# A two-layer kernel on one core: row norms by halves, the root on ScalarE, a Newton step on VectorE

## The chip, the core and the metric

One core of a Trainium2 chip runs the whole program. The time is that of the device for one execution, in microseconds; a median of several runs is given. TensorE (PE) does matmuls and transposes, ScalarE (ACT) functions by table, VectorE (DVE) element-wise work, GpSimd (POOL) the same more slowly, SyncE (SP) issues most transfers. Each engine runs its own instructions in order and waits on semaphores for the others.

## The reference

Two layers on 256 rows of 1024 floats, float32 throughout. What the change touches is the row norm, which stands at six places:

```python
def rmsnorm(x, g):
    y = xf * lax.rsqrt(jnp.mean(xf * xf, axis=-1, keepdims=True) + EPS)
    return (y * g).astype(x.dtype)

h = rmsnorm(x, g_pre)                       # "x"; the projections h @ w_in follow
cross_mixer(q, z, rmsnorm(mem, g_mem), ...) # "m"
x = x + rmsnorm(merged @ w_o, g_post)       # "wo", and the residual sum: end of layer 1
h = rms_norm(x, mix_norm_gain)              # "y": layer 2 begins, projections follow
x = x + mixed @ w_out
h = rms_norm(x, ffn_norm_gain)              # "f": gate/up projections and w_down follow
out = rms_norm(x + ffn, final_norm_gain)    # "o"
```

Between these stand gated linear attention, sparse and cross attention in layer 1, and a gated delta rule with a convolution, block-compressed attention and a feed-forward part in layer 2.

## The kernel before

The 256 rows are two row tiles (t = 0, 1) of 128 partitions by 1024 columns; `xres` holds the residual rows and `xn` the normed or scratch rows. A product with fp32 accuracy is made of three matmuls (L486 to L488): activations and weights are each split into a rounded high part and a low rest. The weights stream through a ring of five slots, a "unit" of up to 2048 columns at a time. For each unit ACT writes the high part (`highs`, L1288) and DVE the low one (`lows`, L1762), in the order of the list `splits`, some two units ahead of PE. `highs(n)` and `lows(n)` do what is missing up to the nth; `bank_ready(name)` does this for two units beyond the bank's own and then waits for the bank. `step(ins)` lets an engine wait for its own instruction.

Products of 512 columns fill the eight PSUM banks in a fixed rotation. A product of row tiles t and column half c has the name `wo<c><t>` (w_o), `w2o<c><t>` (w_out) or `wd<c><t>` (w_down): half 0 of both row tiles is finished first, then half 1.

A norm goes through four engines. ACT squares 1024 columns of one row tile and sums them (`squares`, L1271, instruction at L1273) once all are there; POOL turns the sum into mean plus epsilon (L1665) and raises it to -1/2 (L1666); DVE scales the row tile (`scale_rows`, L1788, instruction at L1791); PE transposes both row tiles (`transpose_tokens`, L542, L551), eight transposes of 128 columns each; the first bank is full after two of the second row tile's. ACT and DVE then write high and low parts of the transposed rows (`high_of_transposed`, L1305; `low_of_transposed`, L1793). PE's order has nothing between the product before a norm and the transposes behind it, except at "m".

In the middle ACT copies the four banks of w_o into `xn` (L1303), squares, and POOL makes the factor of "wo". DVE multiplies by factor and gain (L2046) and adds to `xres` (L2047), and on that sum the "y" norm is made. Behind it ACT has Exp of a small tile (L1497), the high parts of units c1 and c2, and the copies into the convolution, whose taps DVE does at L2099 and L2101. At "f" and "o" DVE adds the banks to `xres` (L2352, L2381) and the norm follows; at the end it multiplies by factor and gain (L2385), and SP stores each row tile (L1234), 512 KB, as it is ready. The order of all this is written out by hand on each engine.

## Time and profile before

| | us |
|---|---|
| median of 3 runs | 953.02 (952.66 to 954.28) |
| the profiled execution | 951.25 |
| its span, first to last instruction | 949.5 |

| Engine | busy us | share |
|---|---|---|
| PE | 907.9 | 96% |
| DVE | 560.5 | 59% |
| ACT | 427.4 | 45% |
| POOL | 60.6 | 6% |

Busy time says which engine works; what ends last is read from the chain of waits. In a timeline a row gives the start, the time from the first start to the last end, the engine, the line and the shape, and in brackets how long the engine had been idle and who released it. Lines are those of the kernel before.

### The profile page before, as it was taken

To read this page: it belongs to the slowest core of one execution; us is meant where nothing else is said; L and a number is where in the kernel's file an instruction comes from. 1 tells how busy PE (TensorE), PEld (TensorE's weight loads), DVE (VectorE), ACT (ScalarE), POOL (GpSimd) and SP (SyncE) were. 2 spreads that over 40 slices of the span, in tenths; PEclk is the share of its full clock that TensorE was granted. 3 is DMA by queue.
4 is the path that set the end of the run, shared out by engine and by line. 5 is a ranking of instruction groups with operands and counts; after the bars stand their busy time and mean duration, and the time that the engine had idled before them with its cause. 6 is when DMAs were issued, how large, how long until landed. Compare 5 with 4: busy or idle time off the path is not lost.

```text
span 949.5 us, 13232 instructions
## 1 busy us (share of the span) xinstructions
PE 907.9 (96%) x5502; PEld 793.6 (84%) x5502; DVE 560.5 (59%) x802; ACT 427.4 (45%) x568; POOL 60.6 (6%) x72
## 2 busy tenths in 40 slices
PE   6999999999999999999699999899989899999996
PEld 5999999899897888887599998677877788888885
DVE  4855564664567565655579786645276555566442
ACT  6644445644346444433554424553443444444341
POOL 1000000000020000000201253000000000000000
PEclk9999999999999999999899999999999999999999
DMA  9657643455264455466567453003563456665441
GB/s 303 196 177 233 201 165 133 134 177 174 94 222 150 161 177 178 152 225 197 165 178 176 91 149 119 1 1 133 133 222 133 155 178 180 191 193 191 155 155 45
DMA packets 127490, 151.77 MB, mean 160 GB/s; under 512 B 16919, under 2 KB 93078, under 8 KB 127430
## 3 DMA queue, kind: packets, MB, share of 16 engines
q1 hardware_dynamic: 127290, 150.83, 50.2%
q8 instruction: 44, 0.72, 0.3%
q14 instruction: 16, 0.13, 0.1%
q0 software_dynamic: 64, 0.07, 0.0%
q10 hardware_dynamic: 76, 0.02, 0.0%
HBM read 148.80 MB, written 3.68 MB: 161 GB/s over the span
## 4 chain that ended last, share of the span: by engine, by line
PE 88%; DVE 8%; ACT 2%; issue 1%; POOL 0%; DMA 0%; ACTq 0%; POOLq 0%; DVEq 0%
PE bank L486 24%; PE bank L487 24%; PE bank L488 24%; DVE w_lo L1762 2%; DVE arena L2101 1%; PE bank L551 1%; PE bank L926 1%; PE bank L957 1%; PE bank L911 1%; PE bank L921 1%; PE bank L731 1%; ACT w_hi L1288 1%; PE bank L900 1%; PE bank L632 1%; PE bank L612 1%
## 5 line engine op out<-in xcount | busy, mean ns | idle before, releaser
L1762 DVE TENSOR_TENSOR w_lo<-ring,w_hi 128x2048 fp32r<-128x2048 f32 (+2 forms) x133 | 299.7, 2258 | 196.6 <-ACT w_hi L1288 196.4
L1288 ACT ACTIVATE w_hi<-ring 128x2048 fp32r<-128x2048 f32 (+2 forms) x133 | 250.0, 1881 | 140.4 <-PE bank L488 128.4
L486 PE MATMUL bank<-h_hi,w_hi 128*128 128x256 f32 (+1 forms) x640 | 184.8, 289 | 2.7 <-DVE w_lo L1762 1.4
L487 PE MATMUL bank<-h_lo,w_hi 128*128 128x256 f32 (+1 forms) x640 | 181.8, 284 | 0.0
L488 PE MATMUL bank<-h_hi,w_lo 128*128 128x256 f32 (+1 forms) x640 | 181.7, 284 | 0.0
L486 PE MATMUL bank<-w_hi,h_hi 128*128 128x512 f32 (+1 forms) x400 | 155.7, 389 | 0.8 <-DVE h_lo L1799 0.8
L488 PE MATMUL bank<-w_hi,h_lo 128*128 128x512 f32 (+1 forms) x400 | 152.7, 382 | 0.0
L487 PE MATMUL bank<-w_lo,h_hi 128*128 128x512 f32 (+1 forms) x400 | 152.5, 381 | 0.0
L486 PEld LDWEIGHTS bank<-h_hi,w_hi 128*128 128x128 f32 (+1 forms) x640 | 123.1, 192 | 5.7 <-issue 3.3
L487 PEld LDWEIGHTS bank<-h_lo,w_hi 128*128 128x128 f32 (+1 forms) x640 | 123.1, 192 | 0.7 <-issue 0.5
L488 PEld LDWEIGHTS bank<-h_hi,w_lo 128*128 128x128 f32 (+1 forms) x640 | 123.0, 192 | 0.0
L1303 ACT ACTIVATE arena<-bank 128x512 f32<-128x512 f32 (+4 forms) x86 | 47.7, 568 | 118.9 <-PE bank L488 95.5
L486 PEld LDWEIGHTS bank<-w_hi,h_hi 128*128 128x128 f32 x400 | 75.2, 188 | 15.9 <-issue 1.8
L488 PEld LDWEIGHTS bank<-w_hi,h_lo 128*128 128x128 f32 x400 | 75.2, 188 | 14.7
L487 PEld LDWEIGHTS bank<-w_lo,h_hi 128*128 128x128 f32 x400 | 75.3, 188 | 13.7
L1335 ACT ACTIVATE arena<-bank 128x512 f32<-128x512 f32 (+1 forms) x48 | 23.9, 500 | 96.5 <-PE bank L488 96.4
L1665 POOL TENSOR_SCALAR arena<-arena 128x1 f32<-128x1 f32 (+2 forms) x17 | 5.3, 313 | 678.0 <-ACT arena L1273 378.1
L486 PE MATMUL bank<-w_hi,y_hi 128*128 128x512 f32 x96 | 39.0, 406 | 1.2 <-DVE w_lo L1762 1.2
L487 PE MATMUL bank<-w_lo,y_hi 128*128 128x512 f32 x96 | 37.9, 395 | 0.0
L1456 ACT ACTIVATE arena<-arena 128x128 f32<-128x128 f32 (+1 forms) x48 | 21.3, 445 | 36.6 <-DVE arena L1978 36.6
L488 PE MATMUL bank<-w_hi,y_lo 128*128 128x512 f32 x96 | 37.7, 393 | 0.0
L487 PE MATMUL bank<-w_lo,f_hi 128*128 128x512 f32 x88 | 35.1, 399 | 0.0
(312 smaller groups left out, 1270.3 us busy)
## 6 DMA issues: line engine op xcount, KB each, us to landing
ring<-in_w_in SPq DMA_DIRECT2D x60, 1024.0 KB, 4.9
ring<-in_w_gate_up SPq DMA_DIRECT2D x44, 512.0 KB, 4.6
ring<-in_w_down SPq DMA_DIRECT2D x10, 1024.0 KB, 5.0
ring<-in_w_mem_kv SPq DMA_DIRECT2D x8, 1024.0 KB, 7.1
ring<-in_w_gla_out SPq DMA_DIRECT2D x4, 1024.0 KB, 4.9
ring<-in_w_x_out SPq DMA_DIRECT2D x4, 1024.0 KB, 5.0
ring<-in_w_dsa_out SPq DMA_DIRECT2D x4, 1024.0 KB, 5.1
ring<-in_w_o SPq DMA_DIRECT2D x4, 1024.0 KB, 5.0
```

What stands on the lines that cost most here:

```text
L486: mm(o, ah, bh, start=start, stop=False, skip_group_check=True)
L487: mm(o, ah, bl, start=False, stop=False, skip_group_check=True)
L488: return mm(o, al, bh, start=False, stop=stop, skip_group_check=True)
L551: ins = nc.tensor.transpose(bank_of(f"T{tag}{j}")[:, 256 * kk + 128 * t:256 * kk + 128 * t + 128], src[:, t, 128 * k:128 * k + 128], ident)
L612: ins = mm(bank[:, 256 * t:256 * t + 256], xq[:, 2 * h + c, 128 * t:128 * t + 128], mk[:, 2 * h + c, :], start=c == 0, stop=c == 1)
L632: ins = mm(bank[:, 256 * c:256 * c + 256], mv[:, m, at:at + 128], probT[:, h % 3, 256 * m:256 * m + 256], start=m == 0, stop=m == 1)
L731: ins = nc.tensor.transpose(bank[:, a:a + 128], rows[:, a:a + 128], ident)
L1288: act(w_hi[:, k % NHI, 0:m], ring[:, order.index(name) % NSLOT, 0:m], ACT.Copy)\
L1303: act(dst, src, ACT.Copy, scale=1.0 if scale is None else scale).then_inc(inc or bank_reader(name), 1)
L1335: act(tnh[:, i % 2, 0:n], src, ACT.Tanh, scale=0.5).then_inc(inc or signal("tanh_done"), 1)
L1456: ins = act(v, v, ACT.Exp, bias=neg_max[:, c:c + 1], scale=-1.0, accum_out=p_sum[:, c:c + 1])
L1762: tt_(w_lo[:, i, 0:m], ring[:, i, 0:m], w_hi[:, k % NHI, 0:m].bitcast(F), ALU.subtract)\
```

## The change

For x and m: ACT squares a row tile as before and then takes the square root of mean plus epsilon itself; DVE makes the same mean, the reciprocal of the root, and one Newton step as a correction factor (1.5 - 0.5 r v r), and scales by both factors in one instruction. The wait for and copy of the parameters `par0` moves behind x's scaling on DVE, and ACT waits for it.

For wo, y, f and o: the sum of squares comes in two halves of 512 columns. The first half's mean (`first_half`, DVE) is the bias under the second half's root. For wo the squares are read from the banks, ACT's copies go, DVE multiplies each bank by the gain (`wo_gain`), and factor and residual sum are one instruction for each half. At the end the gain is multiplied in before the factor is known, and each row tile is scaled and stored in two halves, four transfers of 256 KB. `load_root_table` is a root of no use that stands early, so that the table is there. POOL's work for these norms goes; it writes the constant `eps`. SP's store of the middle rows waits for four halves (`x_mid` 4). Left out below: the counts of waits, POOL's removed lines (one is shown), and the definition of `eps`.

```diff
+                act(p_inv[:, col + t:col + t + 1], sumsq[:, col + t:col + t + 1], ACT.Sqrt, scale=1 / D, bias=eps)\
+                    .then_inc(signal(f"root_{tag}"), 1)
+            square_count = {}
+            def half_squares(tag, src, col, c, t):
+                n = square_count[tag] = square_count.get(tag, 0) + 1
+                i = col + 2 * c + t
+                act(probT[:, c, :], src, ACT.Square, accum_out=sumsq[:, i:i + 1]).then_inc(signal(f"sumsq_{tag}"), 1)
+                sc.wait_ge(signal(f"sumsq_{tag}"), n)
+            def root(tag, col, t):
+                sc.wait_ge(signal(f"first_{tag}"), t + 1)
+                act(p_inv[:, col + 2 + t:col + 3 + t], sumsq[:, col + 2 + t:col + 3 + t], ACT.Sqrt, scale=1 / D,
+                    bias=var[:, col + t:col + t + 1]).then_inc(signal(f"root_{tag}"), 1)
+            def load_root_table():
+                step(act(p_inv[:, 15:16], eps, ACT.Sqrt))
...
+            sc.wait_ge(signal("eps"), 1)
             for t in range(TT):
                 squares("x", xres, 0, t, (signal(f"x_in{t}"), 16))
             highs(1)
+            sc.wait_ge(*read("par0"))
...
-            copy_wide("wo0", xn, 0)
-            for t in range(TT):
-                copy(f"wo1{t}", xn[:, t, 512:1024])
-                squares("wo", xn, 4, t, read(f"wo1{t}"))
-            highs(splits_by["wo11"] + 2)
-            for t in range(TT):
-                squares("y", xres, 0, t, (signal("x_mid"), t + 1))
+            def y_squares(t):
+                for c in range(2):
+                    sc.wait_ge(signal("x_mid"), 2 * t + c + 1)
+                    half_squares("y", xres[:, t, 512 * c:512 * c + 512], 0, c, t)
+                root("y", 0, t)
+            for t in range(TT):
+                bank_ready(f"wo0{t}")
+                half_squares("wo", bank_of(f"wo0{t}")[:, :], 4, 0, t)
+            load_root_table()
+            for t in range(TT):
+                bank_ready(f"wo1{t}")
+                half_squares("wo", bank_of(f"wo1{t}")[:, :], 4, 1, t)
+                root("wo", 4, t)
+                if t == 0:
+                    highs(splits_by["wo11"] + 2)
+            for t in range(TT):
+                y_squares(t)
...
-            highs(splits_by["w2o11"] + 2)
-            for t in range(TT):
-                squares("f", xres, 4, t, read(f"w2o1{t}"))
+            load_root_table()
+            highs(splits_by["w2o01"] + 2)
+            for c in range(2):
+                for t in range(TT):
+                    sc.wait_ge(*read(f"w2o{c}{t}"))
+                    half_squares("f", xres[:, t, 512 * c:512 * c + 512], 4, c, t)
+                    if c == 1:
+                        root("f", 4, t)
+                highs(splits_by["w2o11"] + 2)
...
+            load_root_table()
             highs(len(splits))
-            for t in range(TT):
-                squares("o", xres, 6, t, read(f"wd1{t}"))
+            for c in range(2):
+                for t in range(TT):
+                    sc.wait_ge(*read(f"wd{c}{t}"))
+                    half_squares("o", xres[:, t, 512 * c:512 * c + 512], 0, c, t)
+                    if c == 1:
+                        root("o", 0, t)
...
-                rsqrt_mean("o", 6 + t, 1, D, t + 1)
...
-            def rstd_of(tag, col, t):
-                ve.wait_ge(signal(f"rstd_{tag}"), t + 1)
-                return rstd[:, col + t:col + t + 1]
+            def rstd_of(tag, col, t, n, before):
+                i = slice(col + t, col + t + 1)
+                ve.wait_ge(signal(f"sumsq_{tag}"), n)
+                if before is not EPS:
+                    ve.wait_ge(signal(f"first_{tag}"), t + 1)
+                step(tsc(var[:, i], sumsq[:, i], 1 / D, before, ALU.mult, ALU.add))
+                ve.wait_ge(signal(f"root_{tag}"), t + 1)
+                step(nc.vector.reciprocal(rstd[:, i], p_inv[:, i]))
+                step(stt(p_sum[:, i], rstd[:, i], var[:, i], rstd[:, i], ALU.mult, ALU.mult))
+                step(tsc(p_sum[:, i], p_sum[:, i], -0.5, 1.5, ALU.mult, ALU.add))
+                return rstd[:, i], p_sum[:, i]
+            def scale_tile(tag, src, dst, col, t, n, before):
+                r, correction = rstd_of(tag, col, t, n, before)
+                tsc(dst[:, t, :], src[:, t, :], r, correction, ALU.mult, ALU.mult).then_inc(signal(f"scaled_{tag}"), 1)
+            def first_of(col, t):
+                return var[:, col + t:col + t + 1]
+            def first_half(tag, col, t, n):
+                ve.wait_ge(signal(f"sumsq_{tag}"), n)
+                tsc(var[:, col + t:col + t + 1], sumsq[:, col + t:col + t + 1], 1 / D, EPS, ALU.mult, ALU.add)\
+                    .then_inc(signal(f"first_{tag}"), 1)
 
             def scale_rows(tag, dst, src, col):
                 for t in range(TT):
-                    r = rstd_of(tag, col, t)
-                    tsc(dst[:, t, :], src[:, t, :], r, None, ALU.mult).then_inc(signal(f"scaled_{tag}"), 1)
+                    scale_tile(tag, src, dst, col, t, t + 1, EPS)
...
+            scale_rows("x", xn, xres, 0)
             ve.wait_ge(*full("par0"))
             nc.vector.tensor_copy(par[:, 0:38], bank_of("par0")[:, 0:38]).then_inc(reader("par0"), 1)
             ve.wait_ge(*read("par0"))
             tsc(g_gla_half, g_gla, 0.5, None, ALU.mult)
-            scale_rows("x", xn, xres, 0)
...
+            def wo_gain(c, t):
+                s = slice(512 * c, 512 * c + 512)
+                tt_(xn[:, t, s], bank_of(f"wo{c}{t}")[:, :], g_post[:, s], ALU.mult).then_inc(reader(f"wo{c}{t}"), 1)
+            def x_in_the_middle(t):
+                r, correction = rstd_of("wo", 6, t, 3 + t, first_of(4, t))
+                step(tt_(r, r, correction, ALU.mult))
+                for c in range(2):
+                    s = slice(512 * c, 512 * c + 512)
+                    ve.wait_ge(*read(f"wo{c}{t}"))
+                    stt(xres[:, t, s], xn[:, t, s], r, xres[:, t, s], ALU.mult, ALU.add).then_inc(signal("x_mid"), 1)
+            ve.wait_ge(signal("g_post_in"), 16)
+            for t in range(TT):
+                bank_ready(f"wo0{t}")
+                first_half("wo", 4, t, t + 1)
+                wo_gain(0, t)
             lows(splits_by["wo11"] + 2)
-            ve.wait_ge(signal("g_post_in"), 16)
             ve.wait_ge(signal("x_again"), 16)
             for t in range(TT):
-                r = rstd_of("wo", 4, t)
-                step(stt(xn[:, t, :], xn[:, t, :], r, g_post, ALU.mult, ALU.mult))
-                tt_(xres[:, t, :], xres[:, t, :], xn[:, t, :], ALU.add).then_inc(signal("x_mid"), 1)
-            scale_rows("y", xn, xres, 0)
+                ve.wait_ge(signal("sumsq_wo"), 3 + t)
+                wo_gain(1, t)
+                x_in_the_middle(t)
+                first_half("y", 0, t, 2 * t + 1)
+                if t == 1:
+                    ve.wait_ge(signal("x_mid"), 4)
+                    scale_tile("y", xres, xn, 2, 0, 2, first_of(0, 0))
+            scale_tile("y", xres, xn, 2, 1, 4, first_of(0, 1))
...
+                    if c == 0:
+                        first_half("f", 4, t, t + 1)
             ve.wait_ge(*read("w2o11"))
-            lows(splits_by["Tf3"] + 2)
-            scale_rows("f", xn, xres, 4)
+            for t in range(TT):
+                scale_tile("f", xres, xn, 6, t, 3 + t, first_of(4, t))
...
+                    ve.wait_ge(*read(f"wd{c}{t}"))
+                    step(tt_(xn[:, t, s], v, g_fin[:, s], ALU.mult))
+                    if c == 0:
+                        first_half("o", 0, t, t + 1)
+                    else:
+                        r, correction = rstd_of("o", 2, t, 3 + t, first_of(0, t))
+                        for half in range(2):
+                            o = xn[:, t, 512 * half:512 * half + 512]
+                            tsc(o, o, r, correction, ALU.mult, ALU.mult).then_inc(signal("result"), 1)
```

## Rows read from the trace of the kernel before

**Rows 1.** The page's first part: busy time, share of the span, instructions of each engine.
```profile
PE 907.9 (96%) x5502; PEld 793.6 (84%) x5502; DVE 560.5 (59%) x802; ACT 427.4 (45%) x568; POOL 60.6 (6%) x72
```

**Rows 2.** Waits of PE, whole span: us in total, times, longest us.
```profile
PE bank L551 <- DVE arena L1791: 10.8, 3, 7.2
```

**Rows 3.** Timeline, first 12 us, ACT then DVE: start us, us, instruction, [idle before].
```profile
3.06 1.28 ACT L1273 ACT_TABLE_LOAD   x1 [3.06 <-issue]
5.40 0.19 ACT L1273 ACTIVATION_READ_ACCUMULATOR arena<-arena 128x1 f32 x1
6.01 1.06 ACT L1273 ACTIVATE arena<-arena 128x1024 f32<-128x1024 f32 x1 [0.42 <-DMA arena<-in_x]
...
7.44 0.75 DVE L1791 TENSOR_SCALAR arena<-arena 128x1024 f32<-128x1024 f32 x1
8.63 0.75 DVE L1791 TENSOR_SCALAR arena<-arena 128x1024 f32<-128x1024 f32 x1 [0.44 <-POOL arena L1666]
```

**Rows 4.** Chain that ended last, 7 to 12 us: start us, us, what.
```profile
8.24 2.41 PE bank L551 x10
```

**Rows 5.** Timeline of DVE, two dependent small instructions, 486 us.
```profile
486.56 0.17 DVE L2062 TENSOR_TENSOR arena<-arena 128x8 f32<-128x8 f32 x1
486.76 0.17 DVE L2063 SCALAR_TENSOR_TENSOR arena<-arena 128x8 f32<-128x8 f32 x1
```

**Rows 6.** Timeline of ACT around one table load, 484 to 487 us.
```profile
484.75 1.28 ACT L1512 ACT_TABLE_LOAD   x1
486.04 0.21 ACT L1512 ACTIVATE arena<-arena 128x8 f32<-128x8 f32 x1
```

**Rows 7.** Groups of ACT by line, the table loads: busy us, mean ns | idle before.
```profile
L1406 ACT ACT_TABLE_LOAD x1 | 1.3, 1283 | 0.0
L1411 ACT ACT_TABLE_LOAD x1 | 1.3, 1283 | 0.0
```

**Rows 8.** Timeline at the middle norms: DVE, ACT, DVE.
```profile
456.08 2.29 DVE L1762 TENSOR_TENSOR w_lo<-ring,w_hi 128x2048 fp32r<-128x2048 f32 x1 [5.89 <-ACT w_hi L1288]
...
459.73 0.60 ACT L1303 ACTIVATE arena<-bank 128x512 f32<-128x512 f32 x1 [1.08 <-PE bank L488]
...
465.97 0.75 DVE L1791 TENSOR_SCALAR arena<-arena 128x1024 f32<-128x1024 f32 x1 [0.44 <-POOL arena L1666]
```

**Rows 9.** Groups of DVE by line and form: busy us, mean ns | idle before.
```profile
L2352 DVE TENSOR_TENSOR arena<-arena,bank 128x512 f32<-128x512 f32 x4 | 2.7, 682 | 1.4 <-PE bank L488 1.4
```

**Rows 10.** Timeline after the middle norms: ACT, then DVE.
```profile
472.21 0.25 ACT L1497 ACTIVATE arena<-arena 128x4 f32<-128x4 f32 x1
472.49 1.92 ACT L1288 ACTIVATE w_hi<-ring 128x2048 fp32r<-128x2048 f32 x1
...
474.54 4.49 DVE L1762 TENSOR_TENSOR w_lo<-ring,w_hi 128x2048 fp32r<-128x2048 f32 x2 [1.11 <-ACT w_hi L1288]
480.81 0.62 DVE L2099 TENSOR_SCALAR arena<-arena 128x256 f32<-128x256 f32 x2 [1.78 <-ACT arena L1303]
```

**Rows 11.** Timeline of DVE before the feed-forward norm.
```profile
747.99 0.69 DVE L2352 TENSOR_TENSOR arena<-arena,bank 128x512 f32<-128x512 f32 x1 [0.70 <-PE bank L488]
749.49 0.75 DVE L1791 TENSOR_SCALAR arena<-arena 128x1024 f32<-128x1024 f32 x1 [0.82 <-POOL arena L1666]
```

**Rows 12.** Timeline of DVE at the end.
```profile
941.61 0.69 DVE L2381 TENSOR_TENSOR arena<-arena,bank 128x512 f32<-128x512 f32 x1 [0.71 <-PE bank L488]
...
945.11 1.28 DVE L2385 SCALAR_TENSOR_TENSOR arena<-arena 128x1024 f32<-128x1024 f32 x1 [0.72 <-POOL arena L1666]
```

**Rows 13.** The output tile's transfers (512 KB each).
```profile
DMA to landing us min/median/max: 2.6/2.8/3.0
```

**Rows 14.** Chain that ended last: the same 16 matmuls of L957 twice.
```profile
597.80 1.45 PE bank L957 x16
...
610.94 2.76 PE bank L957 x16
```

**Rows 15.** Windows: us, busy of PE, PEld, DVE, ACT, POOL, granted clock, DMA share, GB/s.
```profile
610.50:613.50 3.00, 3.00 (x20) 1.67 (x16) 1.98 (x12) 1.85 (x8) 0.00 (x0) 0.50 0.00 0
```

30 lines of the change are left out of this document (11 added, 19 removed).

## Prediction

> **What bounds the kernel now.** I read the page's busy times first: TensorE (PE) is busy 96% of the span [rows 1]. Then the waits of PE: the longest group is 10.8 us in three waits, for DVE's scaling by the row norm at L1791 [rows 2]. Then, at each of these places, the chain that ended last and the timeline of each engine. From about 18 us on PE is the engine that ends last nearly everywhere (not in the convolution after the middle, which begins at 480.81 [rows 10] and is DVE's), so whatever a norm gives or takes there goes one to one into the time, unless a later stage absorbs it. Four places count: the norm of x at the start, the two norms between the layers ("wo" and "y"), the one before the feed-forward part ("f") and the output ("o"). The norm of the memory rows ("m") lies under the matmuls of iq0, and it keeps that cover: what it gains in ACT work is two root instructions, some 0.5 us.
>
> A rule for reading them: the 16 transposes that follow a norm run 10 in 2.41 us, 0.24 each [rows 4], and eight of them need only row tile 0. So PE's restart is set by the end of the first scaling, as long as the second ends less than some 1.7 to 1.9 us later.
>
> **Prices.** A small DVE instruction that waits for the one before it takes 0.20 us from start to start [rows 5]. A table load takes 1.28 us and its function runs 0.01 us behind it [rows 6]. A square root of 128x1 is not in the trace; bounds are 0.21 [rows 6] and 0.60, a whole 128x512 bank [rows 8]; I take 0.27, near the 0.25 of L1497 [rows 10]. A bank times a row of gains is 0.68 (L2352 [rows 9]), a half of the fused residual sum the same. A half Square is 0.60 (a bank read by ACT [rows 8]) and its accumulator read 0.19 [rows 3], some 0.1 of it overlapped, 0.7 in all. The scaling of 1024 columns by one column takes 0.75 [rows 8]; now two columns are multiplied. The bounds are 0.75 and 1.28, which the general three-operand form takes for 1024 columns [rows 12]; I take 0.75, since the instruction stays TENSOR_SCALAR.
>
> **Start (x).** ACT reads the accumulator of tile 0 until 5.59 [rows 3]. The load at 3.06 [rows 3] served Square, Copy, Tanh and Exp until the Ln of L1406 [rows 7], so the root needs another one. 5.62 + 1.28 + 0.27 = 7.19. The variance on DVE is done meanwhile; reciprocal, two steps of the correction and the waits are 3 x 0.20 from 7.23; the scaling runs 7.83 to 8.58, where it ran 7.44 to 8.19 [rows 3]. Tile 1: Square of 1.06 from 7.1, accumulator, root until 8.58, scaling 9.22 to 9.97, 1.4 us after the first, so the transposes hide it. Sum: +0.39 us. The move of the copy of par0 behind it costs nothing: the copy ends near 10.2 and its reader, ACT's h_hi, would start at 11.0.
>
> ACT's load back to the Tanh set falls ahead of zx0's tanh at about 110 us, and the pieces after it are two units ahead of PE: nothing. POOL loses its norm work, which PE no longer waits for.
>
> **Middle (wo, y).** ACT's four copies out of the banks go (0.60 each), and so do POOL's powers. Everything on half 0 happens under PE's work on half 1: nothing. The load of the root's table comes right after the two first half Squares (about 449 us) and pushes only the split of beta, wanted 20 us later. The end is DVE's own queue. It can't begin before the low part of c0, which ends at 458.37 [rows 8], because the change leaves that in front. Then: gain of half 1 and variance, 0.8; reciprocal, stt, tsc, product, 4 x 0.20 = 0.80; that is 459.9. Two halves of the fused sum, 1.3, to 461.2. DVE then waits in first_half for ACT's first half Square of y, which begins at 460.70 after the Square and root of wo11 (459.73 + 0.60 + 0.1 + 0.27): 461.45. Everything of tile 1 is queued behind this wait: gain 0.7, five small 1.0, sums 1.3, first_half 0.35, to 464.8. Only then comes tile 0's norm: four small, 0.80, and its scaling, 465.52 to 466.27, where it was 465.97 to 466.72 [rows 8]. Tile 1's ends at 467.75, again 1.5 us later, hidden. Sum: -0.45 us. The 7 us that look free are mostly filled with DVE's serial work, which replaces that of POOL and ACT.
>
> What this starts: the Exp of L1497 needs its table back, 1.28 us on ACT ahead of the high parts of c1 and c2. They start at 472.49 [rows 10]; then at 472.49 - 0.45 + 1.28 = 473.3. DVE's two low parts (4.49 us to 479.03 [rows 10]) end near 479.8, and the convolution starts at 480.81 - 0.45 = 480.36 [rows 10]. So 0.5 us of cover is left: nothing. Without it each further 0.1 counts, since the convolution is on the chain.
>
> **Feed-forward norm (f).** First halves are hidden; they delay the second add of half 0 by 0.4 and the high part of gu0a by 1.8, which is wanted 15 us later. The add of w2o10 ends at 747.29 (0.70 before 747.99 [rows 11]); half Square and root on ACT to 748.35. DVE adds w2o11 until 748.68 in any case, then four small, 0.80, and scales at 749.52; it was 749.49 [rows 11]. The 0.4 us saved on ACT and POOL is eaten by DVE's order. Sum: +0.03. The load for gu0's tanh costs it 0.6 us, under PE's work.
>
> **End (o).** The first add ends at 940.90 (0.71 before 941.61 [rows 12]). Gain 0.7, variance (after ACT's Square at 941.65), root at 942.0, three small: halves of 0.48 (an estimate: 0.75 x 1/2 and a fixed 0.1) from 942.62 to 943.52. The second add, which ran at 941.61, is queued behind them: 943.45. Its Square and root end at 945.20, three small, halves end at 946.33 and 946.75. The last row tile ended at 946.39 [rows 12]. So the last transfer is issued 0.36 us later, but has 256 KB where 512 KB took 2.8 us [rows 13]. Half the size may save nothing to 1.4 us; another quarter goes out 0.4 us before it, so I take 0.4. Sum: 0.0, with bounds -1.0 and +0.4.
>
> **The sum.** 0.39 - 0.45 + 0.03 + 0.0 = about -0.03 us. The profiled execution took 951.25 us with a span of 949.5; this gives 951.2. Against the median of 953.02, 1.8 above the profiled one, it is 953.0.
>
> **Two rules against the rows.** The sum takes a load between x's Square and its root. The rows show a load for Ln at L1406 and another for the next Exp at L1411 [rows 7]: each serves what comes next, with no look ahead. The Trainium skill ("ScalarE activation tables: per-element evaluation and per-set limits", section "Table sets in the compiler and the runtime") says that loads go by the set with the longest run of following functions, and its page "ScalarE: Activation LUTs" ("Table sets: the hidden batching unit") names one set with Ln and Exp; by both there would be one load where the rows show two. By this rule the first load would be the root's: rival A.
> The rows show 1.28 us and no gap [rows 6]. "ScalarE: Activation LUTs" ("What ACT_TABLE_LOAD costs") adds a drain of 1.38 us, 2.66 in all; by that the sum would be +1.4 at the start and +0.9 at the convolution. No row here shows that drain.
>
> **Rivals.** A: the first load already holds the root. Then x's first scaling starts 1.27 us earlier than in my sum; DVE's low of "small" gives some of it back: 0.8 earlier than before, in all -1.3, 951.7. For it: nothing in rows; against it: rows 7. 8%.
> B, slower: DVE multiplies by two columns at the slow pace, 1.28 for 0.75 [rows 12]. First scalings at x, y and f +0.53 each, and the last two halves +0.27 each: +2.1, 955.1. It decides from a scaling above 0.75 on. For it: no row with two columns; against it: every TENSOR_SCALAR on SBUF here is at the fast pace. 5%.
> C, slower: a switch of table costs twice its row (2.56). +1.28 at x, and 0.8 at the convolution beyond its cover of 0.5: +2.1, 955.1. It decides at the convolution from 1.8 us on. Rows 6 speak against it. 4%.
> D: the granted clock. 16 matmuls of L957 take 1.45 us, and 2.76 where the clock is at 0.50, that is 1.2 GHz [rows 14, 15]. Such a stretch may come or go once with the shifts, f's transposes included: 951.7 or 954.3. 14%, both halves alike.
> E, faster: the middle's handovers overlap and the change does what its halves suggest: DVE's small steps cost half there (18 on the path, -1.8), at x, f and the end 3 or 4 each (-1.1): 950.1. For it: POOL, which worked beside DVE there, is silent now; against it: rows 5, which were taken with POOL idle. 8%.
> That nothing is gained since the chains only change engines is my forecast itself: 61%.
>
> **Range and chances.** The forecast reaches from 951.3 to 954.8 by the bounds of the end (-1.0, +0.4), the root (0.21 to 0.60, twice on the path, +0.7) and the spread of the runs. With A and D inside and B, C and E outside, the range is 951.0 to 954.9. A measurement of this kernel can't tell less than 0.2%, 1.9 us. Faster by more: E, and a quarter of A and D, 0.13. Slower by more: B and C and a little of D, 0.10. Same: 0.77.
>
> **What would show it.** Right: a table load between ACT's first two Squares at about 5.6 us; PE's first transpose at 8.6; in the middle PE's wait for L1791's successor 6.8 us where it was 7.2; first f scaling within 0.1 us of 749.5 less the shift; 12 table loads in all. Wrong: two-column scalings of over 0.8 us, a convolution that waits for low parts, a PE wait in the middle under 6 us, or a last transfer that lands over 1 us earlier.

## The result: 3 us slower, where no change was forecast

The changed kernel takes 955.75 us (median of 9 runs, 952.53 to 957.58) where the kernel before took 952.9 in the same comparison (9 runs). The ratio is 1.0027, 95% interval 1.0014 to 1.004; a second comparison, below, gave 1.0035 (1.0020 to 1.0049). So it is slower by about 0.3%, and 955.75 lies outside the range of 951.0 to 954.9. The profiled execution took 956.9 us with a span of 954.8 and a mean granted clock of 0.983, beside 951.25, 949.5 and 0.987 before.

The page of the changed kernel, busy times, which answer to [rows 1]. PE has the same work; DVE has 12 us more and ACT 13 more, POOL 12 less:

```profile
PE 909.0 (95%) x5502; PEld 795.1 (83%) x5502; DVE 572.9 (60%) x870; ACT 440.1 (46%) x602; POOL 48.2 (5%) x49
```

The waits of PE (us in total, times, longest), which answer to [rows 2]: the norms cost it 13.2 us where it was 10.8, and w_lo at the start 4.1:

```profile
PE bank L551 <- DVE arena L1833: 13.2, 4, 7.4
...
PE bank L486 <- DVE w_lo L1797: 4.1, 3, 2.1
```

**The start.** Timeline of the changed kernel, ACT, then DVE, then PE (start us, us, instruction, [idle before]), which answers to [rows 3, 4]:

```profile
4.42 1.28 ACT L1275 ACT_TABLE_LOAD   x1 [4.42 <-DMA arena<-in_x]
5.72 1.06 ACT L1275 ACTIVATE arena<-arena 128x1024 f32<-128x1024 f32 x1
...
6.89 1.28 ACT L1278 ACT_TABLE_LOAD   x1
8.18 0.29 ACT L1278 ACTIVATE arena<-arena 128x1 f32<-128x1 f32 x1
...
9.23 0.81 DVE L1833 TENSOR_SCALAR arena<-arena 128x1024 f32<-128x1024 f32 x1
...
10.10 3.68 PE L551 MATMUL bank<-arena 128*128 128x128 f32 x16 [2.92 <-DVE arena L1833]
...
19.80 0.39 PE L486 MATMUL bank<-h_hi,w_hi 128*128 128x256 f32 x1 [2.08 <-DVE w_lo L1797]
```

The first table load, which in the kernel before ran from 3.06 on while x was still under way, now waits for x and starts at 4.42. The second load follows, as predicted, but 1.3 us late. PE's first transpose comes at 10.10, 1.86 us later than before, and the wait for w_lo passes this on: the matmul that waits for it starts at 19.80, and at 17.89 in the kernel before.

**The middle, f and the end.** ACT's reading of wo11's bank, the first scaling of y, PE; then the last add ahead of f and its first scaling; then the end. They answer to [rows 8, 11, 12]:

```profile
463.07 0.60 ACT L1287 ACTIVATE arena<-bank 128x512 f32<-128x512 f32 x1 [1.78 <-PE bank L488]
...
466.89 1.41 DVE L2106 SCALAR_TENSOR_TENSOR arena<-arena 128x512 f32<-128x512 f32 x2 [0.27 <-DVE arena L2102]
...
469.43 0.81 DVE L1833 TENSOR_SCALAR arena<-arena 128x1024 f32<-128x1024 f32 x1
...
470.39 3.65 PE L551 MATMUL bank<-arena 128*128 128x128 f32 x16 [7.35 <-DVE arena L1833]
...
751.40 0.69 DVE L2425 TENSOR_TENSOR arena<-arena,bank 128x512 f32<-128x512 f32 x1 [0.70 <-PE bank L488]
...
753.01 0.81 DVE L1833 TENSOR_SCALAR arena<-arena 128x1024 f32<-128x1024 f32 x1
...
945.13 0.69 DVE L2458 TENSOR_TENSOR arena<-arena,bank 128x512 f32<-128x512 f32 x1 [6.94 <-PE bank L488]
...
948.62 0.68 DVE L2458 TENSOR_TENSOR arena<-arena,bank 128x512 f32<-128x512 f32 x1
...
951.13 1.00 DVE L2467 TENSOR_SCALAR arena<-arena 128x512 f32<-128x512 f32 x2
```

Read each place from its own start, so that what came earlier drops out. Middle: first scaling of y 6.36 us after ACT starts on wo11 (6.24 before). f: 1.61 us after the start of the last add (1.50 before). End: last result at 951.13 + 1.00, which is 7.00 us after the start of wd10's add (6.18 before), and the span ends 9.67 after it (9.29 before). Together 0.6, and 1.9 from the start: 2.5 of the 5.3 us by which the two spans differ. The rest goes with the slow stretches of the clock.

**The clock.** PE's granted clock falls to 0.50 in stretches of some 3.5 us, 1.7 us of full clock lost in each, or two or three of them in a row. One that costs 1.7 to 2.8 us of full clock lies behind PE's last matmul in every profile, where it costs nothing. The windows (us, busy of PE, PEld, DVE, ACT, POOL, granted clock, DMA share, GB/s) show one near 21 us that the profile of before lacks; first the changed kernel, then the kernel before:

```profile
21.00:24.00 3.00, 3.00 (x16) 3.00 (x15) 2.86 (x7) 2.59 (x3) 0.00 (x0) 0.50 1.10 349
```

```profile
21.00:24.00 3.00, 3.00 (x26) 2.87 (x25) 2.50 (x2) 2.60 (x3) 0.46 (x1) 1.00 1.10 349
```

These stretches come and go from run to run of one kernel: the kernel before had clocks from 0.981 to 0.991 in 100 runs and times from 947.8 to 955.0. So three numbers are used below beside the time. The **product** is a run's span times its mean granted clock; the **loss** is the span less the product. The product isn't the time without the slow stretches, since part of a stretch lies over PE's waits and costs nothing there: in the kernel before it goes from 934.8 at a clock of 0.981 (4 runs) to 937.7 at 0.991 (9 runs), a span 0.74 us longer for each 0.001 of clock, and not the 0.95 that the product takes off. It scatters by 0.3 to 0.7 us within most kernels, where the time scatters by 1 to 2, but it moves with the mix of clocks. The clock is recorded to 0.001, which is 0.95 us of product.

The column **at equal clock** avoids this: each run's span less the mean span of the kernel before at the same recorded clock (less a straight line through its 100 runs, where it has fewer than three at that clock), and the mean of that. At one clock the spans of the kernel before have a standard deviation of 0.25 us at most, so these are good to some 0.3 us, the rounding of the clock included. For the kernels with matmuls of no use neither number serves (in brackets): those matmuls take away stretches that cost little, so they raise both while the time falls.

Means over all runs (median in the third column; the last two columns are the mean of the kernel before in the same comparison and the ratio of the times with its 95% interval):

| kernel | runs | median | mean | product | loss | at equal clock | before, mean | ratio |
|---|---|---|---|---|---|---|---|---|
| before, all comparisons | 100 | | 952.1 | 936.8 | 13.5 | | | |
| changed | 9 | 955.75 | 955.5 | 938.5 | 14.9 | +2.4 | 953.0 | 1.0027 (1.0014-1.0040) |
| a_again: changed | 10 | 954.97 | 955.2 | 939.3 | 13.9 | +2.5 | 951.9 | 1.0035 (1.0020-1.0049) |
| e1_eps_later | 12 | 952.93 | 953.0 | 937.7 | 13.2 | +0.9 | 952.7 | 1.0008 (0.9989-1.0027) |
| e2_root_table_first | 12 | 952.50 | 952.5 | 936.7 | 13.8 | -0.1 | 952.7 | 0.9999 (0.9981-1.0017) |
| e3_old_x | 12 | 953.28 | 953.2 | 937.3 | 14.1 | +0.5 | 952.7 | 1.0012 (0.9996-1.0028) |
| e4_fill | 12 | 954.66 | 954.1 | 943.6 | 8.5 | (+5.7) | 952.7 | 1.0019 (1.0003-1.0035) |
| b_fill | 10 | 950.39 | 950.5 | 941.9 | 6.7 | (+3.7) | 951.9 | 0.9986 (0.9967-1.0004) |
| g1_end | 12 | 952.61 | 952.4 | 936.6 | 13.8 | -0.3 | 951.9 | 1.0007 (0.9994-1.0020) |
| g4_mid_end | 12 | 952.11 | 952.2 | 935.8 | 14.4 | -0.9 | 951.9 | 1.0004 (0.9989-1.0020) |
| c1_before_wait | 12 | 952.52 | 952.7 | 937.4 | 13.5 | +0.5 | 951.5 | 1.0019 (1.0005-1.0033) |
| h1_all | 12 | 951.30 | 950.9 | 940.2 | 8.6 | (+2.4) | 951.5 | 0.9991 (0.9975-1.0006) |
| d1_mid_f | 12 | 952.53 | 952.6 | 936.4 | 14.4 | -0.2 | 952.0 | 1.0009 (0.9998-1.0020) |
| d2_f_end | 12 | 953.27 | 952.8 | 937.2 | 13.9 | +0.4 | 952.0 | 1.0004 (0.9990-1.0018) |

Over its 19 runs the changed kernel is 3.2 us above the kernel before (955.4 and 952.1): 2.5 at equal clock, 0.2 that lies outside the span (2.0 us between span and time, 1.8 before), and some 0.6 for a lower mean clock (0.9849 for 0.9858, uncertain by 0.4 us). The 2.5 is what the four places came to in the trace.

### The profile page after: what moved, and what is told of

Same layout as the page of the kernel before. It is cut to its first block, busy times and chain, and to the rows that moved or that the text cites. A ratio compares the mean times of both kernels' runs of the same rounds, so it can differ in the third digit from the quotient of the medians.

```text
span 954.8 us, 13343 instructions
## 1 busy us (share of the span) xinstructions
PE 909.0 (95%) x5502; PEld 795.1 (83%) x5502; DVE 572.9 (60%) x870; ACT 440.1 (46%) x602; POOL 48.2 (5%) x49
## 4 chain that ended last, share of the span: by engine, by line
PE 88%; DVE 8%; ACT 2%; issue 1%; DMA 0%; DVEq 0%; ACTq 0%
PE bank L486 24%; PE bank L487 24%; PE bank L488 24%; DVE w_lo L1797 2%; DVE arena L2174 1%; PE bank L926 1%; PE bank L911 1%; PE bank L921 1%; PE bank L731 1%; PE bank L551 1%; PE bank L900 1%; PE bank L632 1%; PE bank L612 1%; PE bank L957 1%; PE bank L938 1%
## 5 line engine op out<-in xcount | busy, mean ns | idle before, releaser
L1326 ACT ACTIVATE arena<-bank 128x512 f32<-128x512 f32 (+4 forms) x82 | 45.1, 567 | 113.4 <-PE bank L488 90.4
L487 PEld LDWEIGHTS bank<-w_lo,h_hi 128*128 128x128 f32 x400 | 75.7, 189 | 13.8
L486 PE MATMUL bank<-w_hi,f_hi 128*128 128x512 f32 x88 | 34.8, 395 | 0.0
```

Of the source, the lines that this page charges most:

```text
L486: mm(o, ah, bh, start=start, stop=False, skip_group_check=True)
L487: mm(o, ah, bl, start=False, stop=False, skip_group_check=True)
L1326: act(dst, src, ACT.Copy, scale=1.0 if scale is None else scale).then_inc(inc or bank_reader(name), 1)
```

## Experiments

### What the start costs

Theory 1 says that the start costs 1.9 us since the first table load lost its cover; theory 2, that the slow stretches of the clock decide; theory 3, that DVE's longer serial work in the middle and at the end does. In the changed kernel two waits stand ahead of the first Square, for the column `eps` and for x. The trace shows that `eps` was long written (POOL's constants are done by 0.85 us) and that the load was released by the landing of x. I take it that the wait for x stands ahead of the load in the built program, and that with one wait it stood behind the load, in the Square itself; the profile shows when the load ran, not where a wait was put.

**e1_eps_later** moves one wait of the changed kernel:

```diff
-            sc.wait_ge(signal("eps"), 1)
             for t in range(TT):
                 squares("x", xres, 0, t, (signal(f"x_in{t}"), 16))
...
                 sc.wait_ge(signal(f"sumsq_{tag}"), t + 1)
+                if tag == "x" and t == 0:
+                    sc.wait_ge(signal("eps"), 1)
                 act(p_inv[:, col + t:col + t + 1], sumsq[:, col + t:col + t + 1], ACT.Sqrt, scale=1 / D, bias=eps)\
```

> The changed kernel with one wait moved: ACT waits for eps behind its first Square, ahead of the first root, and no longer ahead of the Square. Theory 1 (lost cover): the wait for x, which stood in the Square, was pushed ahead of the table load, so that the first load (1.28 us) no longer runs while x is in flight. Then the load starts near 3.1 us again, the first scaling 1.28 us earlier than in the changed kernel, PE's first transpose near 8.8 where it was 10.10, and the time falls by 1.3 us against the changed kernel, to about 954.5, unless clock episodes move. Theory 2 (clock): the start is of no account, the episodes of half clock near 21 and in the middle are what costs; the time stays at 955 to 956 while those episodes stay, and falls by 3 or more if the one near 21 us goes.

Its timeline, ACT and PE:

```profile
3.06 1.28 ACT L1275 ACT_TABLE_LOAD   x1 [3.06 <-issue]
...
5.77 1.28 ACT L1280 ACT_TABLE_LOAD   x1
7.06 0.29 ACT L1280 ACTIVATE arena<-arena 128x1 f32<-128x1 f32 x1
...
8.98 3.68 PE L551 MATMUL bank<-arena 128*128 128x128 f32 x16 [1.88 <-DVE arena L1834]
```

The load is at 3.06 again and PE's first transpose at 8.98, 1.12 us sooner. The span falls by 1.3 to 1.5 us at each clock that both kernels have (the product by 1.2, from 938.9, the mean of the 19 runs, to 937.7) and the mean time by 2.4. This is theory 1's size (1.3); that the time fell by more is put down to the clock's scatter, which theory 2 names but which no property of this kernel explains. The second load starts at 5.77, right behind the accumulator read, and the root 0.01 us behind it: as in [rows 6], no drain beside the 1.28 us. The 2.66 us in all that the Trainium skill's page "ScalarE: Activation LUTs" gives (section "What ACT_TABLE_LOAD costs") doesn't show.

**e2_root_table_first** adds one root behind the wait for eps, so that one load serves both functions:

```diff
             sc.wait_ge(signal("eps"), 1)
+            load_root_table()
```

> The changed kernel with one instruction more: ACT takes a square root of the eps column right behind the wait for eps, so that the root's table is in place before the Squares. Theory 1 (the start costs one load that is not covered and a second one between Square and root): both loads' cost goes, since a single load then runs under the transfer of x. First root near 6.9, PE's first transpose near 7.5 where it was 10.10 in the changed kernel and 8.24 before; time 2.6 us under the changed kernel, about 953.1, and PE still waits for w_lo near 18 us for less. If Square were not in the root's set, a load would stand between them again and nothing would be gained. Theory 2 (clock): time follows the sum of the episodes, whatever the start does.

```profile
3.20 1.28 ACT L1298 ACT_TABLE_LOAD   x1 [3.20 <-issue]
...
5.91 0.29 ACT L1278 ACTIVATE arena<-arena 128x1 f32<-128x1 f32 x1
...
6.95 0.81 DVE L1834 TENSOR_SCALAR arena<-arena 128x1024 f32<-128x1024 f32 x1
...
7.82 3.67 PE L551 MATMUL bank<-arena 128*128 128x128 f32 x16 [0.47 <-DVE arena L1834]
```

There is no load between Square and root: the root's table serves Square too. PE starts at 7.82, 0.4 us sooner than in the kernel before (expected: 0.7), and 2.3 sooner than in the changed kernel. The product is 2.2 under the changed kernel's and equal to before; at equal clock it is 2.5 under and again equal. So one line takes back all that the start as changed costs, 1.9 us at PE, and 0.4 more, which pays for the other places.

**c1_before_wait** adds a wait alone to the kernel before:

```diff
+            sc.wait_ge(signal("pool_step"), 1)
             for t in range(TT):
                 squares("x", xres, 0, t, (signal(f"x_in{t}"), 16))
```

> The kernel before with one wait more and nothing else: ACT waits for POOL's first step (a constant that is written within the first microsecond) ahead of its first Square. Theory 1: with two waits the one for x is taken ahead of the table load and the load loses its cover. Then the load starts near 4.4 us where it was 3.06, PE's first transpose comes near 9.6 where it was 8.24, w_lo and the matmuls behind it follow by 1.2 to 1.4, and the time rises by 1.3 to about 953.5 to 954. Rival: the load of the first table is not held by a wait for other data, and starts at 3.1 us as before; then nothing changes.

ACT, then DVE, then PE:

```profile
4.54 1.28 ACT L1273 ACT_TABLE_LOAD   x1 [4.54 <-DMA arena<-in_x]
...
7.13 0.20 DVE L1814 COPY arena<-bank 128x38 f32<-128x38 f32 x1 [7.13 <-PE bank L559]
...
8.01 0.75 DVE L1792 TENSOR_SCALAR arena<-arena 128x1024 f32<-128x1024 f32 x1 [0.48 <-POOL arena L1667]
...
8.82 3.67 PE L551 MATMUL bank<-arena 128*128 128x128 f32 x16 [1.73 <-DVE arena L1792]
```

The wait, for something written long before, moved the load from 3.06 to 4.54: this is shown by itself. In all 14 profiles the load starts at 4.42 to 4.62 where a second wait stands ahead of the wait for x (changed, a_again, e4_fill, c1), and at 3.05 to 3.20 where none does or where the load belongs to an instruction ahead of it (the others). The two waits in the other order weren't tried. But PE came only 0.58 us later, not 1.3. The kernel before, POOL and DVE:

```profile
6.03 0.55 POOL L1666 TENSOR_TENSOR arena<-arena 128x1 f32<-128x1 f32 x1
...
7.13 0.20 DVE L1813 COPY arena<-bank 128x38 f32<-128x38 f32 x1 [7.13 <-PE bank L559]
```

The row factor was ready at 6.58, and the first scaling, at 7.44, was held by DVE's copy of par0, which waits for a transpose of PE. That is 0.8 us of slack which I had not seen. The time rose by 1.2 us in mean (953.5 to 954 was expected, 952.7 came), the span at equal clock and the product by 0.5, as PE's start has it.

**e3_old_x** puts the norms of x and of the memory rows back (POOL's power, one-column scaling, the copy of par0 in front) and leaves middle, f and end as changed. With the root the wait for eps goes from the start, so this undoes all of the start and not the wait alone:

```diff
-                act(p_inv[:, col + t:col + t + 1], sumsq[:, col + t:col + t + 1], ACT.Sqrt, scale=1 / D, bias=eps)\
-                    .then_inc(signal(f"root_{tag}"), 1)
...
-            sc.wait_ge(signal("eps"), 1)
             for t in range(TT):
                 squares("x", xres, 0, t, (signal(f"x_in{t}"), 16))
...
+            for t in range(TT):
+                rsqrt_mean("x", 0 + t, 1, D, t + 1)
+            for t in range(TT):
+                rsqrt_mean("m", 2 + t, 1, D, t + 1)
...
-                    scale_tile(tag, src, dst, col, t, t + 1, EPS)
+                    ve.wait_ge(signal(f"rstd_{tag}"), t + 1)
+                    tsc(dst[:, t, :], src[:, t, :], rstd[:, col + t:col + t + 1], None, ALU.mult)\
+                        .then_inc(signal(f"scaled_{tag}"), 1)
```

> The changed kernel with the norms of x and of the memory rows as they were before (POOL's power, one-column scaling, copy of par0 in front); middle, feed-forward norm and output as changed. Theory 1: the start costs 1.9 us and the other three places together 0.5 (middle +0.2, feed-forward norm -0.05, end +0.4); so 953.4, PE's first transpose at 8.24 again and PE's last matmul some 1.9 us earlier than in the changed kernel. Theory 2 (clock): the episode near 21 us is set off by PE's late start; it goes with it and the middle's falls back to 3.4 us lost, so the time is at or under that of before, up to 2 us more than the start alone. Theory 3 (the longer serial work of DVE in the middle and at the end is the cause): the time stays at 955 or more.

953.2 in mean, as theory 1 says (953.4); at equal clock 1.9 under the changed kernel, which is the start's 1.86, and 0.5 above the kernel before. Theory 3 falls as the main cause; 0.5 us is its part. By theory 2 the stretch near 21 us was to go and the middle to fall back to two; the first did in this profile, but three in a row still lay over the middle.

### What the other places cost

**d1_mid_f** has only middle and f changed, **d2_f_end** only f and end; the rest is the kernel before. (Both are e3_old_x with one more place put back, the end in d1_mid_f and the middle in d2_f_end, with ACT's, POOL's and SP's part of it.) Of the difference to e3_old_x a few lines on DVE, first for d1_mid_f, then for d2_f_end:

```diff
...
-                        for half in range(2):
-                            o = xn[:, t, 512 * half:512 * half + 512]
-                            tsc(o, o, r, correction, ALU.mult, ALU.mult).then_inc(signal("result"), 1)
...
+                stt(xn[:, t, :], xres[:, t, :], r, g_fin, ALU.mult, ALU.mult).then_inc(signal("result"), 1)
```

```diff
...
-                wo_gain(1, t)
-                x_in_the_middle(t)
...
+                step(stt(xn[:, t, :], xn[:, t, :], r, g_post, ALU.mult, ALU.mult))
+                tt_(xres[:, t, :], xres[:, t, :], xn[:, t, :], ALU.add).then_inc(signal("x_mid"), 1)
```

> The middle and the feed-forward norm as changed, everything else (x, memory rows, output) as in the kernel before. By the profiles of the changed kernel the middle costs 0.1 to 0.2 us where I predicted a gain of 0.45, and the feed-forward norm nothing to 0.1. Then y's first scaling starts 6.36 us after ACT begins to read wo11's bank (6.24 in the kernel before), the first scaling of the feed-forward norm 1.61 after the start of the last add (1.50 before), and the span times its clock is 0.1 to 0.3 above that of the kernel before (936.8). By my prediction's -0.45 and +0.03 it would be 0.4 below.

> The feed-forward norm and the output as changed, everything else (x, memory rows, the middle) as in the kernel before. By the profiles the end costs 0.4 us: last result 7.0 us behind the start of the add of wd10 (6.18 before), last landing 0.4 us later. Then the span times its clock is 0.4 to 0.5 above that of the kernel before. By my prediction the end is 0.0; if smaller transfers made up for the later result, the product would be that of the kernel before.

d1_mid_f, its ACT on wo11 and its first scaling of y, 6.12 us apart:

```profile
461.18 0.60 ACT L1283 ACTIVATE arena<-bank 128x512 f32<-128x512 f32 x1 [1.78 <-PE bank L488]
...
467.30 0.81 DVE L1829 TENSOR_SCALAR arena<-arena 128x1024 f32<-128x1024 f32 x1
```

That is 0.12 under the kernel before, and the changed kernel's 6.36 has 0.24 more: a pause ahead of tile 1's sum (the [0.27 idle] at 466.89 above), which is absent here. The pause is in the trace of each kernel with the new norm of x and this middle (changed, a_again, e1, e2, g1: 6.35 to 6.36) and in neither of the two with the old one (e3: 6.13, d1: 6.12), so it goes with the new norms of x and m, far ahead of it. Why is open. The product is 0.5 under that of before, but much of that is its mix of clocks; at equal clock the span is 0.2 under, with an uncertainty of some 0.3. So the middle gave 0.1 by the trace, my expectation of a loss wasn't borne out, and a gain isn't shown either. f starts 1.62 us behind the last add's start, 0.12 later than before. d2_f_end: last result 7.00 us behind wd10's add, product 0.3 and span at equal clock 0.4 above before (expected 0.4 to 0.5). This profile also answers theory 2's question for the start; x is as before, and yet:

```profile
17.83 0.39 PE L486 MATMUL bank<-h_hi,w_hi 128*128 128x256 f32 x1 [2.07 <-DVE w_lo L1791]
```

The wait for w_lo of 2.1 us, and a slow stretch at 19.0 to 23.0 behind it, are here without the new start. The matmuls ahead of that wait ran at the full pace in some profiles and at half pace in others, with 1.00 in the clock's column either way, first the kernel before, then the changed one (256 columns, 0.21 and 0.12 us from start to start):

```profile
13.14 0.41 PE L488 MATMUL bank<-h_hi,w_lo 128*128 128x256 f32 x1
13.35 0.41 PE L486 MATMUL bank<-h_hi,w_hi 128*128 128x256 f32 x1
```

```profile
15.52 0.28 PE L488 MATMUL bank<-h_hi,w_lo 128*128 128x256 f32 x1
15.64 0.28 PE L486 MATMUL bank<-h_hi,w_hi 128*128 128x256 f32 x1
```

Where PE was quick there, it waited 2.05 to 2.09 us for w_lo, and a slow stretch came after (changed kernel, a_again, e2, g1, d1, d2, b_fill); where it was slow, it waited 0.6 us or less and no stretch came there (before, e1, e3, e4_fill, g4, c1, h1). This holds in all 14 profiles, and kernels with either start are on both sides: the stretch near 21 us isn't a property of the change. What makes PE quick or slow there is open.

**a_again** is the changed kernel once more:

> The changed kernel once more, beside the next three on one chip. From the runs so far the span times its mean granted clock, which takes the slow stretches out, is 938.5 us for the changed kernel and 936.7 for the kernel before, each within 1 us in nearly every run. Theory 1 (structure: start 1.9, middle 0.1 to 0.2, end 0.4): this difference stays at 1.8 to 2.4 and the median at 955 to 956. Theory 2 (the number of slow stretches): the product is the same for both kernels and only the clock differs.

The product was 939.3, 2.5 above before, the span at equal clock 2.5 us above too, and the median 954.97. Theory 2, with equal products, falls; the 0.6 us (uncertain by 0.4) that goes with the mean clock over all 19 runs isn't explained, and may be chance.

### Orders that DVE could run in

**g1_end** is e2 with another order of the same instructions at the end (a list of the steps, not the code; the numbers are row tile and half):

```diff
-            add(wd10) gain(0) small(0) scale(0,0) scale(0,1) add(wd11) gain(1) small(1) scale(1,0) scale(1,1)
+            add(wd10) gain(0) add(wd11) gain(1) small(0) var(1) recip(1) scale(0,0) stt(1) scale(0,1) tsc(1) scale(1,0) scale(1,1)
```

> The kernel with the root's table first, and at the end another order on DVE: the second tile's last sum and both gains run before the small steps, and the small steps of the second tile lie between the scalings of the first. The same work, no instruction more or less. The changed end loses since DVE starts on the second tile only when the first tile's norm is done: in the changed kernel the add of wd11 ran at +3.49 us behind that of wd10, and the last result was ready at +7.00 (+6.18 in the kernel before). If that is its cause, the add comes at +1.4, the last result at +5.7, and the time falls 1.2 us under that of the kernel with the root's table first, to about 951.3. If the end is bound by the transfers instead (four of 256 KB on one queue), it moves by less than 0.4.

```profile
941.29 0.69 DVE L2459 TENSOR_TENSOR arena<-arena,bank 128x512 f32<-128x512 f32 x1 [7.08 <-PE bank L488]
...
942.68 0.69 DVE L2459 TENSOR_TENSOR arena<-arena,bank 128x512 f32<-128x512 f32 x1
...
946.23 1.00 DVE L2493 TENSOR_SCALAR arena<-arena 128x512 f32<-128x512 f32 x2
```

The second add comes at +1.39 and the last result at 946.23 + 1.00, +5.94, 1.06 sooner (+5.7 was expected). But the span ended 9.21 us behind the first add where the changed kernel had 9.67, only 0.46 sooner. The product is 0.2 under e2's, and the mean time, 952.4, is e2's (951.3 was expected). With four results within 1.8 us the last landing takes longer: a median of 2.6 us from issue to landing, and 2.3 in the changed kernel. So both answers were half right: DVE's order held the last result back by 1.1 us, and the transfers take back 0.6 of what the new order gains there.

**g4_mid_end** adds a new order in the middle, y's tile 0 scaled ahead of tile 1's sums (again a list of steps):

```diff
-            gain(1,1) small(wo,1) sums(1) small(y,0) scale(y,0) small(y,1) scale(y,1)
+            gain(1,1) [small(wo,1), small(y,0) in turns] scale(y,0) sums(1) small(y,1) scale(y,1)
```

> The same, and in the middle DVE scales row tile 0 before it sums tile 1; the small steps of two chains take turns. Same work. In the changed kernel PE's first transpose for y came 7.3 us after ACT began to read wo11's bank. Theory 1 (DVE's serial queue sets the middle): y's first scaling starts 2.5 us earlier, PE's wait falls from 7.35 to 4.9 us, and PE then waits some 3 us for tile 1; its last transpose ends 0.2 to 1.0 us earlier, and so does the convolution; the time is 0.2 to 1.0 under that of the kernel with the new end. Theory 2 (clock): PE runs and waits twice, so the slow stretch moves; its length decides and the time can rise by 1.7.

PE, the transposes of y in the two kernels, g4_mid_end first, then g1_end:

```profile
463.81 1.94 PE L551 MATMUL bank<-arena 128*128 128x128 f32 x8 [4.51 <-DVE arena L2139]
467.71 1.97 PE L551 MATMUL bank<-arena 128*128 128x128 f32 x8 [1.96 <-DVE arena L2139]
470.33 0.43 PE L486 MATMUL bank<-h_hi,w_hi 128*56 128x256 f32 x1 [0.65 <-DVE h_lo L1855]
```

```profile
467.95 3.65 PE L551 MATMUL bank<-arena 128*128 128x128 f32 x16 [7.35 <-DVE arena L1834]
472.25 0.29 PE L486 MATMUL bank<-h_hi,w_hi 128*56 128x256 f32 x1 [0.65 <-DVE h_lo L1855]
```

The wait falls from 7.35 to 4.5 (4.9 expected), and a second of 2 us comes (3 expected). Measured from ACT's start on wo11 (459.33, and 460.64 in g1_end), the first matmul behind the transposes is at +11.0 and +11.6 (+11.5 in the kernel before). The product falls by 0.8, the lowest of all, and is 1.0 under the kernel before, 0.9 at equal clock. The time doesn't follow: 952.2 beside 951.9, with more of the clock lost in these runs.

### Does an idle PE cost clock?

**e4_fill** (on the changed kernel) and **b_fill** (on the kernel before) keep PE busy in its waits for y and f, with matmuls that compute nothing of use:

```diff
+            fills = {"y": (28, mg_hi, mg_lo), "f": (9, m2_hi, m2_lo)}
...
+                n, hi, lo = fills.get(tag, (0, None, None))
+                for i in range(n):
+                    mm(bank_of(f"T{tag}3")[:, :], hi[:, i % 4, 0:128], lo[:, 0:2, :].rearrange("p a b -> p (a b)"),
+                       start=True, stop=True)
```

> The changed kernel with matmuls added that compute nothing of use: 28 of 512 columns ahead of the transposes of y and 9 ahead of those of the feed-forward norm, into banks that the transposes fill later, while PE would wait. Theory 2 (clock): the granted clock falls to 0.50 behind an idle PE; with PE busy through the middle it stays at 1.00 there, and 3 to 5 us come back: 951 to 953. Theory 1 and 3 (the extra work on ACT and DVE is the cause and the clock only scatter): PE's work behind the norms starts as before, the time stays at 955.7, or is above it where the fill ends later than the norm.

> The kernel before with the same extra matmuls as were added to the changed kernel (28 ahead of the transposes of y, 9 ahead of those of the feed-forward norm), which compute nothing of use. Theory 2 (slow stretches behind an idle PE are what the time hangs on): the mean clock rises from 0.985 to 0.990 and 3 us come back, to 950. Theory 1: in the changed kernel the fill raised the mean clock by 0.007 and gave 1 to 1.5 us; most of the slow stretch there lay over PE's idle time and over work that waits for DVE. Then this is 951.5 to 953.

b_fill's y transposes run at the full clock:

```profile
460.96 6.55 PE L550 MATMUL bank<-mg_lo,mg_hi 128*128 128x512 f32 x28
468.27 1.09 PE L557 MATMUL bank<-arena 128*128 128x128 f32 x8 [0.76 <-DVE arena L1797]
```

The loss falls by 5.9 us on the changed kernel (14.4 to 8.5) and by 6.5 on the other, so at these two places most of the slow stretches hang on the idle PE. (In e4_fill's profile one of 3.5 us is left behind each of the two; in b_fill's none is.) The time falls by 1.3 (955.4 to 954.1) and 1.4 (951.9 to 950.5), each uncertain by some 0.6. Of the expectations, 951 to 953 by the clock and 955.7 by the extra work, e4_fill met neither; b_fill's 950.5 lies nearer to the 950 of the clock than to the 951.5 of theory 1. A good part of the slow stretch lay over the wait itself, where it costs nothing: in the profile of the kernel before it ran from 463.5 to 470.5, and PE was idle until 466.87. And what the transposes gain (two times 1.09 us for 3.65) is partly a longer wait for h_lo: in e4_fill the first matmul behind them waits 1.28 us, where it waited 0.65. b_fill has the lowest median of all, but its interval still touches 1.

**h1_all** is g4_mid_end with such matmuls (17 of 512 columns and 22 of 128 at y, 9 at f):

> Everything that helped, together: the root's table first, y's first scaling ahead of tile 1's sums, the new order at the end, and matmuls that compute nothing of use in PE's waits for the two norms (17 of 512 columns and 22 of 128 at y, 9 of 512 at the feed-forward norm). The span times its clock of the version without them was 935.8, 1.0 under that of the kernel before (936.8), with no fewer slow stretches; the fill alone brought the kernel before down by 1.4 us in mean (950.5 beside 951.9). If both add up, this is 2.4 us under the kernel before, 949.5 to 950.5. If the fill only moves the slow stretches onto work that counts, it stays at 952.

The result is 950.9 in mean, 951.3 in median; the ratio is 0.9991 (0.9975 to 1.0006). The two gains didn't add up: 0.6 us under the kernel before, not 2.4. No version was shown to beat the kernel before.

## Why the prediction was wrong

**Start: wrong, and the largest part.** Predicted +0.39, measured +1.86 at the first transpose. The step that failed is the first one, "ACT reads the accumulator of tile 0 until 5.59": it takes the load at 3.06 and the Square behind it over from the kernel before. The diff adds `sc.wait_ge(signal("eps"), 1)` ahead of that Square, and the sum has no term for it. With it the load ran from 4.42, behind the landing of x, lost its cover of 1.28 us, and the accumulator was read until 6.87. The second load and the root (0.29 for 0.27) were right: with the wait moved (e1_eps_later) the load stood at 5.77 (5.62 forecast) and PE at 8.98 (8.6). The 0.4 that is left there is x landing some 0.15 later in that run, small steps of 0.19 to 0.26, and the scaling's 0.81. None of the rivals held this; B, C and D had the sign and near the size, but other mechanisms.

**Middle: sign open, size wrong.** Predicted -0.45 at the first scaling, measured +0.12 in the changed kernel and -0.12 in d1_mid_f. The queue was as I had it. My terms add up to 465.60 for the first scaling and not to 465.52, so it was -0.37 even as written. The rest is that they were too small: DVE's two halves of the sum took 1.42 instead of 1.3, twice; the 14 small steps took 0.19 to 0.26 from start to start, not 0.20; ACT's first half Square of y had to wait for the first half of the sum, which I had not counted, and came 0.1 late; and there was the pause of 0.24, which comes with the new norms of x and m. The wait of PE was to be 6.8 and was 7.35. The cover at the convolution held: ACT's load for Exp ran at 475.83, and DVE waited for ACT's copy out of PE's bank, not for the low parts.

**f: right.** Predicted +0.03, measured +0.11.

**End: at its bound.** Predicted 0.0 with bounds of -1.0 and +0.4; measured +0.4 in the spans, and +0.3 to +0.4 in d2_f_end, product and equal clock. The last result came 0.82 later, not 0.36, since wd11's add was queued until +3.49, not +3.25, the two halves took 1.00 and not 0.90, and the steps between took 0.1 more. Half the size landed 0.4 us sooner, which is what I took.

**Two-column scaling, rival B.** 0.81 us where one column took 0.75: not the slow form of 1.28, but above the 0.75 that I took, and just over the 0.8 that I had named as a sign of being wrong. **Rival A** didn't happen by itself; e2_root_table_first made it happen, and it gave 0.4 us at PE and nothing measurable in time, not 1.3. **Rival C** didn't happen. **Rival D**: the stretches came and went as it said, but several per run; in mean some 0.6 us of the 3.2 go with them, uncertain by 0.4. **Rival E** didn't happen. Table loads: 12, as forecast.

With +1.86 for +0.39, nothing for the middle's -0.45 and +0.4 for the end, the same sum gives 953.0 + 1.5 + 0.45 + 0.4 = 955.35, outside the range and near the 955.75 that came. The start alone carries it only to 954.5, inside the range; it took the middle's missing gain and the end as well. The range took in the bounds of each price, and no case in which a wait moved a load.

## What to carry to other kernels

Ask of each added wait what it moves, not only whether it is already fulfilled: here one fulfilled wait ahead of the wait for x sent the table load from 3.06 us to behind the landing of x, 4.42 and 4.54, a whole load of 1.28 us. Where two functions can share a table, as Square and the root did in e2, a call ahead of the data lets one load serve both. This row norm, moved between engines as a chain of dependent small steps, kept its length (6.36 us in the middle for 6.24); what shortened it was the order of the queue, and that only up to the next limit (here the landing of the output, and tile 1's transposes).

## What the runs showed beside this

- The column of the granted clock doesn't show all: matmuls of 256 columns ran 0.21 us apart at 13 to 16 us in the kernel before and 0.12 apart in the changed one, with 1.00 in both, and the 14 profiles divide evenly.
- Spans compared at equal clock separate kernels that the time can't: for the kernels without matmuls of no use they agree within 0.3 us (e1_eps_later: 0.45) with the sum of what the trace shows at the start, in the middle, at f and at the end, where the mean time of 12 runs is uncertain by 0.3 to 0.65. Span times mean clock does so only roughly: for d1_mid_f it showed a gain of 0.5 us that is 0.2 at equal clock.
- Kernels with the new norm of x have 2.0 us between span and time, those with the old one 1.8, in every comparison. Why is open.
